# The last gate of a transformer block with tokens on the partitions

## The reference

```python
    h = h + 0.5 * swiglu(rms_norm(h, ffn2_norm[i]), ffn2_w_in[i], ffn2_w_out[i])
    hn = rms_norm(h, ple_norm[i])
    h = h + jax.nn.sigmoid(hn @ ple_w_gate[i]) * (p[i] @ ple_w_proj[i])
return rms_norm(h, final_norm)
```

## Time and profile before

| | us |
|---|---|
| median of 3 runs (lowest, highest) | 3514.57 (3513.77, 3516.12) |
| profiled execution | 3513.87 |
| its span, first to last instruction | 3512.0 |
| mean granted TensorE clock, as a share of full | 0.994 |

### The profile page before, as it was taken

One profiled execution on the slowest core, in us unless ns is written; L12 is line 12 of the kernel. 1 busy time (PEld: TensorE's weight loads), 2 busy tenths in 40 slices (PEclk: granted clock), 3 DMA queues, 4 the chain that ended last, 5 costly groups with the idle time before them and its releaser, 6 DMA issues.

```text
span 3512.0 us, 42997 instructions
## 1 busy us (share of the span) xinstructions
PE 3441.4 (98%) x16552; PEld 2794.9 (80%) x16560; DVE 1989.5 (57%) x3115; ACT 1249.6 (36%) x1827; POOL 924.6 (26%) x388
## 2 busy tenths in 40 slices
PE   7999999999999999999999999999999999999997
PEld 5787787888888888888888887888768888888885
DVE  6889768878888887222222226330568765632205
ACT  3234633223333333322222224332345656333223
POOL 0010243441000000344444444444111000444441
PEclk9999999999999999999999999999999999999999
DMA  3211233333456546655555552222312222322222
GB/s 111 90 60 43 69 118 120 120 123 129 169 179 204 168 163 205 222 195 193 192 192 193 194 195 90 96 96 96 115 61 80 71 79 72 120 96 96 96 90 84
DMA packets 144359, 446.75 MB, mean 127 GB/s; under 512 B 12776, under 2 KB 45928, under 8 KB 139936
## 3 DMA queue, kind: packets, MB, share of 16 engines
q1 hardware_dynamic: 108304, 405.26, 33.8%
q10 hardware_dynamic: 35856, 38.75, 3.2%
HBM read 372.64 MB, written 71.32 MB: 126 GB/s over the span
## 4 chain that ended last, share of the span: by engine, by line
PE 88%; DVE 6%; DVEq 2%; ACT 1%; issue 1%; POOL 1%; DMA 1%; POOLq 0%; SPq 0%; ACTq 0%
PE ps L212 54%; PE ps L1044 19%; PE ps L1340 6%; PE ps L1027 2%; DVE conv_out L754 2%; PE ps L1567 1%; DVEq L741 1%; PE ps L1596 1%; POOL slot_parts L200 1%; PE ps L1540 1%; DVE norm_r L302 1%; PE ps L1682 1%; DVEq L810 1%; ACT slot_parts L196 0%; PE ps L1665 0%
## 5 line engine op out<-in xcount | busy, mean ns | idle before, releaser
L212 PE MATMUL ps<-h_norm_hi,slot_parts 128*128 128x512 f32 x4688 | 1498.1, 396 | 23.3 <-POOL slot_parts L200 9.6
L200 POOL TENSOR_TENSOR slot_parts<-ring,slot_parts 128x1024 fp32r<-128x1024 f32 x371 | 902.3, 2434 | 2270.5 <-ACT slot_parts L196 2270.5
L212 PEld LDWEIGHTS ps<-h_norm_hi,slot_parts 128*128 128x128 f32 x4688 | 882.1, 188 | 223.6 <-POOL slot_parts L200 12.5
L212 PE MATMUL ps<-x_low,slot_parts 128*128 128x512 f32 x2280 | 887.8, 389 | 0.0
L196 ACT ACTIVATE slot_parts<-ring 128x1024 fp32r<-128x1024 f32 x558 | 587.2, 1053 | 482.9 <-DMA ring<-in_stream 297.1
L1044 PE MATMUL ps<-gated_hi,slot_parts 128*128 128x512 f32 x2048 | 631.0, 389 | 1.5 <-POOL slot_parts L200 1.5
L212 PEld LDWEIGHTS ps<-x_low,slot_parts 128*128 128x128 f32 x2280 | 430.1, 189 | 90.2 <-issue 1.0
L1044 PEld LDWEIGHTS ps<-gated_hi,slot_parts 128*128 128x128 f32 x2048 | 384.4, 188 | 81.8 <-POOL slot_parts L200 1.9
L1044 PE MATMUL ps<-gated_lo,slot_parts 128*128 128x512 f32 x1024 | 398.4, 389 | 0.0
L1272 DVE TENSOR_TENSOR gated<-gates_back,experts_back 128x512 f32<-128x512 f32 x128 | 97.4, 761 | 494.5 <-DMA experts_back<-experts_dram 464.6
L200 DVE TENSOR_TENSOR slot_parts<-ring,slot_parts 128x1024 fp32r<-128x1024 f32 x187 | 229.6, 1228 | 140.2 <-ACT slot_parts L196 135.2
(11 more groups left out here) (379 smaller groups left out, 3423.4 us busy)
## 6 DMA issues: line engine op xcount, KB each, us to landing
ring<-in_stream SPq DMA_DIRECT2D x560, 512.0 KB, 3.3
experts_dram<-experts SPq DMA_DIRECT2D x64, 512.0 KB, 4.6
gates_dram<-gates_by_key ACTq DMA_DIRECT2D x32, 1024.0 KB, 10.3
gates_back<-gates_dram SPq DMA_DIRECT2D x32, 1024.0 KB, 4.8
experts_back<-experts_dram SPq DMA_DIRECT2D x64, 512.0 KB, 4.9
x_res<-in_xT SPq DMA_DIRECT2D x2, 2048.0 KB, 9.8
x_dram<-x_res SPq DMA_DIRECT2D x4, 512.0 KB, 3.2
bias_by_distance<-bias_rows_dram ACTq DMA_DIRECT2D x8, 256.0 KB, 4.1
```

What stands on the lines that cost most here:

```text
L200: e.tensor_tensor(to[:, BUFFER[n], 1, :], ring[:, n % RING, :], to[:, BUFFER[n], 0, :].bitcast(F32), ALU.subtract).then_inc(s_lo, 1)
L212: mm = e.matmul(psum, w2[wv][:, k, :], x2[xv], start=start and v == 0, stop=stop and v == 2)
```

## The change

The last gate is computed with tokens on the partitions. Output block b (0 to 7) is 128 tokens (b // 2) x 512 channels (b % 2), one PSUM bank each. The stationary operand is a 128 x 128 piece of `Hh` or `Lo`, the moving operand a row block of the weights, so a slot now holds 128 input channels for all outputs, and all eight banks collect over k at once: 192 matmuls as before. The root is one number per partition, which ACT applies inside the sigmoid, and the last norm's sum of squares comes from ACT's accumulator. The projection moves ahead of the gate; so do its two slots in the stream. TensorE turns `X` into tokens (`x_tokens`, 32 transposes). The final gain is a row, broadcast to all partitions by a DMA. The output is stored by token blocks, and the host no longer turns it. The old `ple_` functions are removed whole (they stand above); `after.py`'s lines are 3 higher from L1358 on.

```diff
@@ STREAM
-    ("f2_in", 44), ("f2_out", 22), ("ple_gate_a", 2), ("ple_proj", 2), ("ple_gate_b", 6),
+    ("f2_in", 44), ("f2_out", 22), ("ple_proj", 2), ("ple_gate", 8),
@@ ffn_act
             tg, tw = f.tmp[:, 2 * (p % 2), :], f.tmp[:, 2 * (p % 2) + 1, :]
             e.wait_ge(f_scaled, f.p0 + p + 1)
             e.activation(tg, tg, ACT.Silu).then_inc(f_gate, 1)
+            if f.n == 2 and p == 2:
+                e.dma_start(pT_[:, :, :], a["pT"].rearrange("(k p) s -> p k s", p=P)).then_inc(e_in, 16)
             slot_hi(e, f.n0 + 2 * p + 4)
             e.wait_ge(f_prod, f.p0 + p + 1)
             e.activation(f.F[0][:, p, :], tw, ACT.Copy).then_inc(f_hi, 1)
             slot_hi(e, f.n0 + 2 * p + 5)
-        for n in range(f.nd + 4, f.nd + FT + 1):
+        for n in range(f.nd + 4, f.nd + FT):
             slot_hi(e, n)
+        slot_hi(e, START["misc" if f.n == 1 else "ple_gate"])
         for k in range(KT):
             e.wait_ge(f_added, f.added0 + k + 1)
             part_hi(e, f.q + 1, k)
@@ the last stage
...
+    BANKS = (1, 2, 3, 4, 5, 6, 7, 0)
+    BANK0 = 2 * (KT - 1)
+    def tok(b):
+        return slice(b // 2 * P, b // 2 * P + P)
+    def chan(b):
+        return slice(b % 2 * S, b % 2 * S + S)
     def ple_pe(e):
         e.wait_ge(e_in, 16)
+        for b in range(KT):
+            e.wait_ge(f_added, ffns[1].added0 + b + 1)
+            for c in range(2):
+                mm = e.matmul(PS[:, b, :], pT_[:, c, tok(b)], slot(e, npj + c)[:, chan(b)], start=c == 0,
+                              stop=c == 1)
+                if b == KT - 1:
+                    mm.then_inc(slot_done, 1)
+            if b < KT - 1:
+                mm.then_inc(f_down, 1)
+        e.wait_ge(x_sum, adds_up_to(3, KT - 1))
+        e.wait_ge(e_pp, 1)
+        for n in range(NB):
+            mm = e.matmul(PS[:, 0, n:n + 1], norm_r[:, n * P:(n + 1) * P], mean[:, 0:1], start=True, stop=True)
+        mm.then_inc(x_mean, 1)
+        for b in BANKS:
+            e.wait_ge(e_pp, b + 1)
+            if b == 0:
+                e.wait_ge(x_root, NROOT[3] + 1)
+            for c in range(4):
+                mm = e.transpose(PS[:, b, c * P:(c + 1) * P], X[:, b % 2 * 4 + c, tok(b)], ident)
+            mm.then_inc(f_down, 1)
+        turns = [(b, k) for k in range(4) for b in (BANKS if k == 0 else range(KT))]
+        turns += [(b, k) for ks in ((4, 5, 6), (7,)) for b in range(2) for k in ks]
+        turns += [(b, k) for b in range(2, KT) for k in range(4, KT)]
+        for b, k in turns:
+            w2 = slot_parts(e, n_pg + k)
+            e.wait_ge(x_lo, 4 * KT + k + 1)
+            if k == 0:
+                e.wait_ge(e_turned, BANKS.index(b) + 1)
+            for y, (wv, xv) in enumerate(THREE):
+                mm = e.matmul(PS[:, b, :], (Hh, Lo)[xv][:, k, tok(b)], w2[wv][:, chan(b)],
+                              start=k == 0 and y == 0, stop=k == KT - 1 and y == 2)
+            if b == (0 if k == 0 else KT - 1):
+                mm.then_inc(slot_done, 1)
+            elif k == KT - 1:
+                mm.then_inc(f_down, 1)
     def ple_act(e):
         e.activation(root_warm[:, :], c_("one"), ACT.Sqrt)
+        e.wait_ge(e_in, 16)
+        e.dma_start(g_row[:, :, :].rearrange("p c s -> p (c s)"), a["final_row"].partition_broadcast(P))\
+            .then_inc(e_in, 16)
+        for b in range(KT):
+            if b < 3:
+                slot_hi(e, n_pg + b + 1)
+            if b < KT - 1:
+                e.wait_ge(f_down, BANK0 + b + 1)
+            else:
+                e.wait_ge(slot_done, npj + 2)
+            e.activation(pp[:, b, :], PS[:, b, :], ACT.Copy).then_inc(e_pp, 1)
+        e.wait_ge(x_mean, NMEAN[3] + 1)
+        e.activation(r_x[:, :], PS[:, 0, 0:NB], ACT.Sqrt, bias=c_("eps")).then_inc(x_root, 1)
+        for k in range(4, KT):
+            slot_hi(e, n_pg + k)
+        e.activation(root_warm[:, :], c_("one"), ACT.Sigmoid)
+        e.wait_ge(x_sum, NADD[4] + 1)
+        def square_y(b):
+            e.wait_ge(e_added, b + 1)
+            e.activation(gt[:, b, :], xT[:, b, :], ACT.Square, accum_out=y_sq[:, b:b + 1]).then_inc(x_sq, 1)
+        def last_roots(n, c):
+            e.activation(root_warm[:, :], c_("one"), ACT.Sqrt)
+            e.wait_ge(x_sum, NADD[4] + 2 + n // 2)
+            e.activation(r_y[:, n:n + c], y_ms[:, n:n + c], ACT.Sqrt, scale=1.0 / D, bias=c_("eps"))\
+                .then_inc(x_root, 1)
+        for b in range(KT):
+            if b < KT - 1:
+                e.wait_ge(f_down, BANK0 + 2 * KT + b)
+            else:
+                square_y(b - 1)
+                e.wait_ge(slot_done, n_pg + KT)
+            e.activation(gt[:, b, :], PS[:, b, :], ACT.Sigmoid, scale=r_x[:, b // 2:b // 2 + 1]).then_inc(e_gate, 1)
+            if 0 < b < KT - 1:
+                square_y(b - 1)
+            if b == 4:
+                last_roots(0, 2)
+        last_roots(2, 1)
+        square_y(KT - 1)
+        e.wait_ge(x_sq, NSQ[4] + KT)
+        e.wait_ge(x_sum, NADD[4] + 4)
+        e.activation(r_y[:, 3:4], y_sq[:, 7:8], ACT.Sqrt, scale=1.0 / D, bias=y_ms[:, 3:4]).then_inc(x_root, 1)
+        e.wait_ge(x_sum, NADD[4] + 5)
+        for b in (4, 5):
+            e.activation(pp[:, b, :], pp[:, b, :], ACT.Copy, scale=r_y[:, 2:3]).then_inc(n_nh, 1)
+        e.wait_ge(n_nh, 3 * KT + 2)
+        e.dma_start(out[tok(4), :], pp[:, 4:6, :].rearrange("p c s -> p (c s)")).then_inc(s_out, 16)
     def ple_pool(e):
+        for k in range(KT):
+            slot_lo(e, n_pg + k)
     def ple_dve(e):
+        for i, b in enumerate(BANKS):
+            e.wait_ge(f_down, BANK0 + KT + i)
+            e.tensor_copy(xT[:, b, :], PS[:, b, :]).then_inc(e_turned, 1)
+        e.wait_ge(x_root, NROOT[3] + 1)
+        e.reciprocal(r_x[:, :], r_x[:, :]).then_inc(x_sum, 1)
+        e.wait_ge(e_pp, KT)
+        e.wait_ge(e_in, 32)
+        def last(n):
+            for c in range(2):
+                o = pp[:, 2 * n + c, :]
+                e.tensor_scalar(o, o, r_y[:, n:n + 1], None, ALU.mult).then_inc(n_h, 1)
+        for b in range(KT):
+            e.wait_ge(e_gate, b + 1)
+            e.tensor_tensor(pp[:, b, :], gt[:, b, :], pp[:, b, :], ALU.mult)
+            e.drain()
+            e.tensor_tensor(xT[:, b, :], xT[:, b, :], pp[:, b, :], ALU.add).then_inc(e_added, 1)
+            e.drain()
+            if b == 4:
+                e.wait_ge(x_sq, NSQ[4] + 4)
+                e.tensor_tensor(y_ms[:, 0:2], view(y_sq[:, 0:1], [2, 2]), view(y_sq[:, 1:2], [2, 2]), ALU.add)\
+                    .then_inc(x_sum, 1)
+            if b == KT - 1:
+                e.wait_ge(x_sq, NSQ[4] + KT - 1)
+                e.tensor_scalar(y_ms[:, 3:4], y_sq[:, 6:7], 1.0 / D, EPS, ALU.mult, ALU.add).then_inc(x_sum, 1)
+            e.tensor_tensor(pp[:, b, :], xT[:, b, :], g_row[:, b % 2, :], ALU.mult)
+            if b == 5:
+                e.wait_ge(x_root, NROOT[4] + 1)
+                e.reciprocal(r_y[:, 0:2], r_y[:, 0:2])
+                e.drain()
+                last(0)
+            if b == 6:
+                last(1)
+                e.wait_ge(x_sq, NSQ[4] + 6)
+                e.tensor_tensor(y_ms[:, 2:3], y_sq[:, 4:5], y_sq[:, 5:6], ALU.add).then_inc(x_sum, 1)
+        e.wait_ge(x_root, NROOT[4] + 2)
         e.drain()
+        e.reciprocal(r_y[:, 2:3], r_y[:, 2:3]).then_inc(x_sum, 1)
+        e.wait_ge(x_root, NROOT[4] + 3)
+        e.reciprocal(r_y[:, 3:4], r_y[:, 3:4])
+        e.drain()
+        last(3)
...
+            for i, (b, n) in enumerate(((0, 2), (2, 2), (6, 1), (7, 1))):
+                e.wait_ge(n_h, 3 * KT + (2, 4, 5, 6)[i])
+                e.dma_start(out[tok(b), b % 2 * S:(b % 2 + n) * S], pp[:, b:b + n, :].rearrange("p c s -> p (c s)"))\
...
```

More of the change, by code:

```diff
@@ L2262, in build @@
     keep(m, 4)
+    pp = sb(m, "p_projected", [P, KT, S])
+    xT = sb(m, "x_tokens", [P, KT, S])
+    gt = sb(m, "ple_gate", [P, KT, S])
+    g_row = sb(m, "final_row", [P, 2, S])
+    r_x, r_y, y_sq, y_ms = [sb(m, "ple_" + x_, [P, n_]) for x_, n_ in (("root", NB), ("last_root", NB),
+                                                                     ("squares", KT), ("mean", NB))]
+    sb(m, "ple_before_p_T", [P, 11244])
     pT_ = sb(m, "p_T", [P, 2, S])
-    pp = sb(m, "p_projected", [P, KT, S])
@@ L2265, in build @@
-    gt = sb(m, "ple_gate", [P, KT, S])
     m.close()
[L2267 to L2270, removed]
-    def ple_pe(e):
[L2273 to L2284, removed]
-        e.wait_ge(e_in, 16)
[L2286 to L2297, removed]
@@ L2299, in ple_act @@
-    def ple_act(e):
[L2300 to L2314, removed]
-        e.activation(root_warm[:, :], c_("one"), ACT.Sqrt)
-        for t in range(KT - 2, KT):
-            e.wait_ge(e_added, t + 1)
-            square(e, 4, t)
-        e.wait_ge(x_mean, NMEAN[4] + 1)
-        e.activation(norm_r[:, :], PS[:, 7, :], ACT.Sqrt, bias=c_("eps")).then_inc(x_root, 1)
+    e_in, e_pp, e_turned, e_gate, e_added = sems("ple_", "in", "proj", "turned", "gate", "out")
@@ L2322, in ple_pool @@
```

(33 more changed lines are left out.)

12 lines of the change are left out of this document (5 added, 7 removed).

## The result

| | before | after |
|---|---|---|
| median of 6 runs each (us) | 3515.07 | 3526.97 |
| lowest, highest | 3513.62, 3516.33 | 3524.89, 3529.68 |
| profiled execution, its span | 3513.87, 3512.0 | 3526.77, 3525.0 |
| mean granted clock | 0.994 | 0.993 |

The ratio of the times is 1.0034, with a 95% interval of 1.0024 to 1.0044: the change costs about 12 us. The forecast was 3526.8.

A forecast was written before the change was run, and what follows sets the result against it. PE, busy 98% of the span, was taken as the bound. PE's end at 3513.2 plus 11.0 us gives span 3524.2 against 3512.0, +12.2; 3514.57 + 12.2 = 3526.8 us, range 3518.0 to 3534.5.

The forecast's parts named there:

- The first hold: In the projection: ACT's copy of gate slot 0 waits until 3434.7, so PE waits for DVE from 3434.9 to 3439.5.
- The loads of slots 2 and 3: Gate slots loaded behind the projection: landing 3.3 and 5.0 us after issue, at 3453.7 and 3456.2, holding ACT's bank copies.
- The price of a transpose: Between projection and gates on PE: 0.87 us a bank, 0.22 each, 7.0 us for all 32.
- Rival B: Transposes run at 1.2 GHz throughout: seven banks take 12.2 us, first gates lose 1.4, time 3532.9; chance 0.23.
- The gates: Last gate on PE: 192 matmuls at 0.229, 43.9 us from 3465.5, plus a 2.8 us wait for slot 7.
- The clock as a whole: Slow clock behind PE's three long waits: 1.4 us for each of the first two, 1.0 for the third.
- The end: From PE's last matmul to the span's end: 11.0 us, bounds 9.5 and 12.5, with ACT's table loads delaying late blocks.
- C: At gate slot 0's load: ACT is not held, gates start at 3459.5, 6.0 us less, 3520.8; chance 0.09.
- D: ACT is held, but waits cost no clock (3.8 less) and POOL doesn't hold DVE (1.65 less): 3521.4; chance 0.13.
- E: Faster: all waits covered, PE ends at 3495.3, 9.5 us behind it, time 3507.4; chance 0.05.

The follow-up runs named there:

- Experiment 1: Changed kernel with ACT's copy of gate slot 0 moved behind the eight parts and squares of X: 3521.88 us, 1.0018 to before.
- Experiment 10: Changed kernel with the broadcast of the gain's row issued behind the root instead of ahead of the slot copies: 3526.30 us, 1.0032 to before.
- experiment 5: Changed kernel with gate slot 0's copy behind the parts of X and bank copies ahead of those of gate slots 1 to 3: 3512.11 us, 0.9995.
- experiment 3: Changed kernel with three blocks instead of two (27 matmuls instead of 18) to cover gate slot 7: 3526.26 us, 1.0028 to before.
- experiment 6: Changed kernel with one root for blocks 0 to 5 behind the last sigmoid, ACT scaling blocks 3 to 5: 3525.96 us, 1.0033 to before.
- experiment 4: Changed kernel with each of the 32 transposes issued twice into the same place: 3529.8 us in one run.
- experiment 2: Changed kernel with ACT's copies of the projection's banks ahead of its copies of gate slots 1 to 3: 3523.17 us, 1.0022 to before.
- experiment 9: The four edits, but the stores of token blocks 0 to 3 (1 MB) left out, arithmetic kept: 3507.50 us, 0.9981 to before.
- the four edits: Changed kernel with gate slot 0's copy late, bank copies first, three blocks covering slot 7, one root: 3510.87 us, 0.9987 to before.

## Why the prediction was right, and where two errors cancelled

**The first hold** went as worked out, step by step: copy of gate slot 0 at 3434.68 (3434.7 forecast), first low part to 3438.72 (3438.85), third addition at 3439.3 (3439.5), PE's wait 4.0 (4.6) with 1.5 for the projection slot before it, last addition at 3448.75 (3448.9), last square sum at 3452.4 (3452.6), projection to 3451.6 (3451.2). Experiment 1 shows the cause: without the copy ahead the wait for DVE is gone, the gates start 4.7 to 7.2 us earlier, by which trace of the same front one compares, and the median falls by 5.1.

**The loads of slots 2 and 3** I took to land 3.3 and 5.0 us behind their issues, with 3453.7 and 3456.2. They took 5.4 and 5.8 and landed at 3456.2 and 3457.5: I had mentioned the broadcast beside them and charged nothing for it. ACT's first wait was therefore already at slot 2, and bank 2's transposes began at 3459.36, 1.4 later than forecast: 0.5 because slot 3's load was issued later (3451.67, not 3451.2), 0.8 because it took 5.8. Experiment 10 puts the broadcast's term at 0.7 to 1.3.

**The price of a transpose** is the step that failed. I read the eight records of the earlier trace rows as four transposes (its heading says so too) and put 0.22 us at full clock. L1611 issues eight; each record is one transpose, and at full clock they go at 0.11 (32 in 3.45 us, experiment 5), so all 32 cost 3.5 us and not 7.0. The second error went the other way: I let the clock be back after 1.4 us of loss, but it stayed at 0.50 from 3454.19 to 3464.43, and the transposes went at 0.21 to 0.22 there. Seven banks took 5.5 us (7.5 forecast). Together with the 1.4 of the loads the gates started at 3464.85, against 3465.5: a near hit for two wrong reasons, and the forecast owes that much to luck. So does the comparison itself: the same instructions started the gates 1.8 and 2.5 us earlier in experiments 3 and 6, whose clock was low there for 6.8 us and not for 10.2.

**Rival B** said that transposes leave the clock low. They did run at the low level nearly to their end, but the rule behind B isn't what the runs show. Between 3461.00 and 3464.40 PE ran transposes alone, and the clock was full at 3464.43, 0.4 us before the first gate matmul; in experiment 4 it rose among transposes and stayed, and in experiments 2, 3 and 6 it also rose among them (in experiment 3 at 3464.09, with transposes from 3460.60 to 3466.29). The Trainium skill, "TensorE: Matmul & The Clock Gate", section "Part 4: PE-mode transpose", says that transposes don't count as PE work for the clock; these traces disagree, at least for float32 transposes of 128 x 128 back to back.

**The gates.** PE waited 2.6 us for slot 7 (2.8). The clock then cost 0.255 - 0.235 = 0.020 us for each of 78 matmuls, 1.6 us (1.0; the bound was 1.4). And a gate matmul took 0.235 from start to start, not 0.229: the chain's piece of the earlier trace rows begins at 3457.40, 0.56 after its first matmul, so I should have divided 33.1 by 143, 0.232. These make PE's end 3514.5 instead of 3513.2.

**The clock as a whole.** Measured at both levels in the traces of the changed kernel and of experiment 5, and counted in records (a projection or small matmul has two): 24 of the projection at 0.507 against 0.433 (1.8 us), 8 small ones at 0.18 against 0.10 (0.6), 28 transposes at 0.215 against 0.11 (2.9), 78 gates (1.6): the records took 6.9 us longer. I had charged 3.8. But not all of the 6.9 moves the end. The small ones end in front of a wait for ACT, and the projection is also paced by DVE's additions: in experiment 6 the clock stayed full there behind a wait of 3.7 us, and the 24 records still took 11.4 us, against 12.3, so the clock cost 0.8 there (window, length, busy PE, PEld, DVE, ACT, POOL, clock, DMA share, GB/s):

```profile
3439.20:3450.70 11.50, 11.30 (x24) 4.23 (x24) 11.04 (x18) 7.83 (x12) 0.00 (x0) 1.00 0.00 0
```

With 2.9 as the upper bound for the transposes, whose banks ACT copies at 0.5 us each, the clock cost this trace at most 5.3 us.

**The end** took 10.5 us (11.0 forecast, bounds 9.5 and 12.5). This too is a sum of two errors: DVE's last scaling ended 6.6 us after PE's last matmul (7.7 forecast), and from there it took 3.9 us (3.3). ACT's first table load began 7.1 us ahead of PE's end, some 0.5 earlier than I put it; the order of table loads, root and sigmoid is the one I had worked out (timeline of ACT):

```profile
3507.45 1.28 ACT L2353 ACT_TABLE_LOAD   x1
3508.74 0.20 ACT L2353 ACTIVATE root_warm<-cst 128x1 f32<-128x1 f32 x1
3508.85 0.28 ACT L2355 ACTIVATE ple_last_root<-ple_mean,cst 128x2 f32<-128x2 f32 x1
3509.15 1.28 ACT L2364 ACT_TABLE_LOAD   x1
3510.44 0.69 ACT L2364 ACTIVATE ple_gate<-ps,ple_root 128x512 f32<-128x512 f32 x1
```

The next ACTIVATE starts 0.01 us behind each load, so the drain that the Trainium skill, "ScalarE: Activation LUTs", section "What ACT_TABLE_LOAD costs", adds isn't seen here either. What I had not seen is that the stores lengthen the end once the compute in front of them is shorter (experiments 6 and 9).

**Rivals C, D and E.** C (ACT not held) and D (holds without cost in clock) are excluded by the copy at 3434.68 and by the windows at 0.50; D's other half, that POOL doesn't hold DVE, by the low part of 2.33 us. But in experiment 6 the first hold alone cost no clock. E, faster, would have needed every wait to be wrong. Yet it is what the change can be made into: with the four edits the gates start at +19.6 and PE ends at +65.5 instead of +84.5.

**Why the edits don't add up.** Each hold at the front starves PE by itself. With the first removed, the banks wait as long as before (4.9 us) and their transposes still run at 0.215; with the second removed, the additions are still late. Only with both removed is there no low clock before the gates, and no wait but the 1.1 us for the projection's second slot. With all four edits PE takes 5.3 us more than before from the FFN's end to its own (65.5 against 60.2), and the end shrinks from 21.6 to 11.1. Experiment 5 differs from the changed kernel only in where `slot_hi` calls stand on ACT, and is not told from before: these calls' places cost 14.9 us, more than the 12 by which the change is slower.

## What to carry to other kernels

When the order of a stream changes, look for every instruction that waits for one of its slots and read what is queued behind it on its engine: a copy that waits delays all that stands behind it. Fix holds together before judging an edit, since here each alone won 5.1 and 3.8 us and both together 14.9, and a wait can cost clock on top of its length. Count how many operations a group of records is by the loop that issues it. Before shortening the compute of an end, look at the stores that would then be issued at once.
